# Linear attention inside a two-block layer: the exponents of the levels s = 32 and 64 taken from the running sum too, and running sums multiplied one head earlier

## What is computed

```python
b = jnp.cumsum(gc, axis=2)
rel = b[:, :, :, None, :] - b[:, :, None, :, :]
decay = jnp.exp(jnp.where(mask, rel, -jnp.inf))
attn = jnp.einsum('bhid,bhjd,bhijd->bhij', qc, kc, decay)
o = jnp.einsum('bhij,bhjv->bhiv', attn, vc) + jnp.einsum('bhid,bhdv->bhiv', qc * jnp.exp(b), state)
```

## Time and profile before

| | |
|---|---|
| median of 3 runs | 2332.88 us (2327.26 to 2337.95) |
| the profiled execution's own time | 2329.45 us |
| its span, first to last instruction | 2327.7 us |
| PE busy | 2269.9 us (98%) |
| DVE busy | 1671.5 us (72%) |
| ACT busy | 1117.6 us (48%) |
| POOL busy | 596.6 us (26%) |
| granted TensorE clock, mean | 0.997 |

### The profile page before, as it was taken

The page is one execution under the profiler, slowest core; times in us unless marked ns, Lnnn a source line. Parts: engine busy times, 40 slices in busy tenths (PEclk is TensorE's granted clock), DMA queues, the critical chain, the costliest instruction groups (busy, mean ns, idle before and its releaser), DMA issues.

```text
span 2327.7 us, 40250 instructions
## 1 busy us (share of the span) xinstructions
PE 2269.9 (98%) x14434; PEld 1352.6 (58%) x14434; DVE 1671.5 (72%) x3037; ACT 1117.6 (48%) x1755; POOL 596.6 (26%) x469
## 2 busy tenths in 40 slices
PE   8999999999999999999999999999999999999998
PEld 4448657555555666655555555564444465445885
DVE  6337765678999899968888888877453458777246
ACT  4267535666566788843333333344422234333234
POOL 0011213777787622233222222113000010000011
PEclk9999999999999999999999999999999999999999
DMA  6300034788888679989999999923333333333322
GB/s 201 93 10 1 2 98 131 247 294 306 310 307 296 219 268 356 355 320 396 372 358 358 364 358 361 368 72 112 92 114 100 100 98 104 100 104 108 101 73 73
DMA packets 164575, 471.26 MB, mean 202 GB/s; under 512 B 16800, under 2 KB 71712, under 8 KB 163680
## 3 DMA queue, kind: packets, MB, share of 16 engines
q1 hardware_dynamic: 109008, 289.94, 37.7%
q0 software_dynamic: 36864, 134.23, 15.5%
q10 hardware_dynamic: 18576, 45.36, 4.9%
HBM read 421.49 MB, written 47.45 MB: 201 GB/s over the span
## 4 chain that ended last, share of the span: by engine, by line
PE 76%; DVE 13%; ACT 3%; DMA 2%; POOL 2%; issue 2%; DVEq 1%; POOLq 0%; SPq 0%; ACTq 0%
PE psum L692 23%; PE psum L694 23%; PE psum L693 23%; DVE arena L2587 3%; DMA arena<-in_urows,arena 2%; DVE arena L666 1%; DVEq L2512 1%; POOL arena L672 1%; PE psum L1211 1%; ACT arena L653 1%; PE psum L1084 1%; PE psum L1379 1%; PE psum L1181 1%; PE psum L1380 1%; POOL arena L3001 1%
## 5 line engine op out<-in xcount | busy, mean ns | idle before, releaser
L692 PE MATMUL psum<-arena 128*128 128x384 f16 (+4 forms) x3968 | 1304.7, 330 | 20.0 <-POOL arena L672 4.9
L693 PE MATMUL psum<-arena 128*128 128x384 f16 (+4 forms) x3968 | 1308.2, 330 | 0.0
L694 PE MATMUL psum<-arena 128*128 128x384 f16 (+4 forms) x3968 | 1301.9, 330 | 0.0
L692 PEld LDWEIGHTS psum<-arena 128*128 128x128 f16 x3968 | 384.6, 97 | 309.5 <-issue 16.7
L694 PEld LDWEIGHTS psum<-arena 128*128 128x128 f16 x3968 | 383.6, 97 | 287.8 <-issue 1.1
L693 PEld LDWEIGHTS psum<-arena 128*128 128x128 f16 x3968 | 383.7, 97 | 278.7 <-issue 0.8
L666 DVE SCALAR_TENSOR_TENSOR arena<-arena 128x1024 f16<-128x1024 f32 x216 | 264.9, 1231 | 250.7 <-ACT arena L653 250.2
L653 ACT ACTIVATE arena<-arena 128x1024 f16<-128x1024 f32 x216 | 226.4, 1051 | 219.8 <-PE psum L694 170.8
L2031 ACT ACTIVATE arena<-arena 128x1024 f16<-128x1024 f32 x128 | 135.3, 1057 | 301.3 <-PE psum L694 287.3
L672 POOL TENSOR_TENSOR arena<-arena 128x1024 f16<-128x1024 f32 x104 | 229.8, 2210 | 78.8 <-ACT arena L661 77.7
L3001 POOL DMA_INDIRECT arena<-in_v,arena x128 | 129.3, 1010 | 359.9 <-DVE arena L2598 328.1
(11 more groups left out here) (290 smaller groups left out, 2275.9 us busy)
## 6 DMA issues: line engine op xcount, KB each, us to landing
arena<-in_w SPq DMA_DIRECT2D x320, 512.0 KB, 3.9
arena<-in_v SPq DMA_DIRECT2D x128, 512.0 KB, 6.0
early_activations<-arena ACTq DMA_DIRECT2D x124, 192.0 KB, 5.2
arena<-early_activations SPq DMA_DIRECT2D x124, 192.0 KB, 6.0
gate_matrix<-arena ACTq DMA_DIRECT2D x5, 4096.0 KB, 18.5
arena<-gate_matrix SPq DMA_DIRECT2D x32, 640.0 KB, 8.3
arena<-in_xT SPq DMA_DIRECT2D x4, 528.0 KB, 5.2
arena<-in_urows,arena POOLq DMA_INDIRECT x128, 6.9
```

Source lines behind the costliest of these rows:

```text
L692: nc.tensor.matmul(ps, a_h, b_h, start=first, stop=False)
L693: nc.tensor.matmul(ps, a_h, b_l, start=False, stop=False)
L694: return nc.tensor.matmul(ps, a_l, b_h, start=False, stop=last)
```

## The change

All seven levels within a tile, 0 to 6, go the way of the running sum (`NARROW` = 7): TensorE no longer multiplies sums for the levels 5 and 6 (16 matmuls a head, 64 in all), and GpSimd subtracts for 7 levels a head instead of 5, in the order of use (`SUB_ORDER`: 6, 0, 1, 2, 3, 4, 5). The running sums of the heads 0 and 1 are multiplied ahead of the levels' loop, that of head h + 2 behind head h. META's sums move from before the first unit of a head to before its third (`ISSUED` {2: META, 5: level 7, 7: level 8}).

```diff
-        NARROW = 5
-        EXP_ORDER = (STEPS[0], PREFIX, *STEPS[1:])
-        AHEAD = (META, NARROW, NS, NS + 1, STEPS[0], PREFIX)
-        PRODUCTS = [(0, STEPS[0]), (0, PREFIX), *((h + n // 4, li) for h in range(HEADS) for n, li in enumerate(AHEAD)
-                                                  if h + n // 4 < HEADS)]
-        ISSUED = {0: 0, 2: 1, 5: 2, 7: 3, 8: 4}
+        NARROW = NS
+        SUB_ORDER = LEVEL_ORDER[:NARROW]
+        EXP_ORDER = [(0, PREFIX), (1, PREFIX)]
+        for h in range(HEADS):
+            EXP_ORDER += [*((h, li) for li in STEPS), *([(h + 2, PREFIX)] if h + 2 < HEADS else [])]
+        AHEAD = (META, NS, NS + 1, PREFIX)
+        PRODUCTS = [(h, li) for h, li in EXP_ORDER if li in AHEAD]
+        ISSUED = {2: META, 5: NS, 7: NS + 1}
...
-                    if i in ISSUED and 2 + 6 * h + ISSUED[i] < len(PRODUCTS):
-                        exponents(2 + 6 * h + ISSUED[i])
+                    if i in ISSUED:
+                        exponents(PRODUCTS.index((h, ISSUED[i])))
...
-                if h < HEADS - 1:
-                    exponents(2 + 6 * h + 5)
+                if h + 2 < HEADS:
+                    exponents(PRODUCTS.index((h + 2, PREFIX)))
...
             turn_copy(HEADS * TT - 2)
-            step_exp(0)
+            prefix_copy(0)
             turn_copy(HEADS * TT - 1)
...
-            prefix_copy(0)
+            prefix_copy(1)
             head_out(HEADS - 1)
...
-            for n in range(1, HEADS * NSTEP + 3):
+            for n in range(HEADS * NSTEP + 3):
                 h, p = divmod(n, NSTEP)
                 if n < HEADS * NSTEP:
                     step_exp(n)
-                    if p == 0:
-                        prefix_copy(h)
+                    if p == NSTEP - 1 and h + 2 < HEADS:
+                        prefix_copy(h + 2)
...
-                for li in range(NARROW):
+                for li in SUB_ORDER:
                     n, s = narrow(h, li) - 1, LEVELS[li]
-                    if li == 0:
+                    if li == SUB_ORDER[0]:
                         pool.wait_ge(e_exp, exped(h, PREFIX))
```

More of the change, by code:

```diff
@@ L778, in exped @@
         def exped(h, li):
-            return h * len(EXP_ORDER) + EXP_ORDER.index(li) + 1
+            return EXP_ORDER.index((h, li)) + 1
         def narrow(h, li):
-            return h * NARROW + li + 1
+            return h * NARROW + SUB_ORDER.index(li) + 1
         keys_in, pq_out, s_done, s_out, head_done, gsub_out, gexp_out = (
@@ L1248, in _ @@
                                  stop=True).then_inc(wide_done, 1)
-            pe.wait_ge(e_exp, HEADS * len(EXP_ORDER))
+            pe.wait_ge(e_exp, exped(HEADS - 1, NS + 1))
             head_sums(1, A[0], range(HEADS - 1))
@@ L1881, in _ @@
                     nc.scalar.activation(xh[:, p // 2, 0:T], otmp[:, p // 2, :], ACT.Copy).then_inc(mixh_out, 1)
-                if p == 0:
+                if p == 0 and h >= 1:
                     pair_copy(h - 1)
@@ L2440, in _ @@
                     if h == 0 and p == 1:
-                        dve.wait_ge(e_exp, exped(0, PREFIX))
+                        dve.wait_ge(e_exp, exped(1, PREFIX))
                         nc.vector.tensor_tensor(KTm[0:DH], gk[0:DH, :, T:TM], v3(Emm, HEADS)[0:DH],
@@ L2982, in _ @@
                     if n >= len(subs):
-                        pool.wait_ge(e_exp, exped(*divmod(n - len(subs), NARROW)))
+                        pool.wait_ge(e_exp, exped((n - len(subs)) // NARROW, SUB_ORDER[(n - len(subs)) % NARROW]))
                     x = paired(prefix[h % 2], s)
```

## The result

The changed kernel takes 2347.47 us (median of 13 runs, 2336.15 to 2354.25), the kernel before took 2332.66 us in the 13 runs beside it (2327.26 to 2341.36): ratio 1.0054 [1.004, 1.0067] (the quotient of the medians, 1.0063, lies in that interval). The forecast was 2332.8 us with an upper end of 2338.5 us: it is wrong, the kernel became slower.

What follows compares the result with a forecast made beforehand. TensorE, busy for 98% of 2327.7 us, was taken as the bound; +1.1 - 0.2 - 0.4 - 0.3 - 0.6 + 0.3 = -0.1 us on the profiled 2329.45, plus 3.43 to the median, gave 2332.8 us, range 2326.5 to 2338.5 us.

Steps and rivals of the forecast that it cites:

- meetings: A POOL subtraction running beside a DVE product: two in head 0 at 0.15 us each, nothing in heads 1 to 3.
- start of head 0, without the hold: Level 6's exponential now needs running sum, copy and subtraction, so head 0's first units run later: +1.1 us.
- end of head 0, start of head 1: Passage from head 0 to 1: -0.2 us for dropped sums, -0.1 us for META's sums replacing level 5's.
- end of head 1, start of head 2: One group of sums dropped, -0.2 us; META's sums moved, -0.1, and ACT's copies sooner, -0.25 us.
- end of head 2, start of head 3: Both groups of sums dropped, -0.2 us; META's sums moved, -0.1, and ACT's copies sooner, -0.35 us.
- their 4.4 us: PE time of the 64 dropped matmuls, 8 groups of 0.55 us; forecast to be mostly not gained.
- Rival A: PE's own time decides, so the dropped sums count in full: -4.3 us, 2328.6 us; chance 0.17.
- POOL beside DVE: Subtractions now fall beside DVE's products: +0.3 us in head 0 (between 0 and 2.1), nothing in heads 1 to 3.
- the forecast's own sign against itself: If the products at line 2348 lengthen beyond 0.9 us, the forecast is wrong and the slower rival holds.
- The cover in heads 1 to 3: DVE's waits for PE at each step (0.17 us in one row) hide meetings, up to about 0.5 us a head.
- rival B: POOL's subtractions hold DVE's products of levels 1, 2 and 3: +3.7 us (2336.5) to +9.6 us (2342); chance 0.16.
- two groups stood around unit 7, of level 6 and of PREFIX: Sums at a head's end; dropping one or both gives -0.2 us, as level 8 waits for DVE.

Runs made afterwards that it cites:

- 1: Changed kernel with GpSimd's 28 subtractions left out, exponentials reading the running sum itself: 2330.46 us, ratio 1.0.
- 7: Changed kernel with head 0's level 6 from TensorE's sums again and each subtraction waiting for DVE's product three before it: 2329.6 us, ratio 0.9996.
- 10: Changed kernel with only the two subtractions a head at the passages between heads waiting for DVE's product: 2335.17 us, ratio 1.0016.
- looks 5 and 6: Changed kernel without any edit, profiled twice more to see slower executions: 2351.31 and 2354.36 us, both at clock 0.987.
- 2: Changed kernel with each subtraction from the fourth on waiting for DVE's product three before it, not for ACT's exponential: 2335.4 us, ratio 1.0009.
- 3: Changed kernel with head 0's level 6 made from TensorE's sums in PSUM again, undoing the late start: 2342.76 us, ratio 1.0053.
- 11: Changed kernel with only the five subtractions a head away from the passages waiting for DVE's product: 2347.18 us, ratio 1.0074.
- 9: Changed kernel with 24 of the 64 dropped matmuls put back at their old places, read by nobody: 2335.8 us, ratio 1.0029.
- look 1: First of two further profiles of the changed kernel, without any edit: 2351.31 us at clock 0.987.

## Why the prediction was wrong

**What held.** Compared with the kernel without meetings (1), the terms come out nearly as summed.

| term | forecast, us | measured, us | from |
|---|---|---|---|
| start of head 0, without the hold | +1.1 | +1.2 | 1 against before, second masked copy (16.91 for 15.71) |
| end of head 0, start of head 1 | -0.2 - 0.1 | -0.36 | head 1 of 1 |
| end of head 1, start of head 2 | -0.2 - 0.35 | -0.65 | head 2 of 1, 7 and after |
| end of head 2, start of head 3 | -0.2 - 0.45 | -0.65 | head 3 of 1, 7 and 10 |

That the sums do not bring their 4.4 us is also right. Rival A is out: the whole of the gain in run 7 is 1.7 us. At the passage from head 1 to 2 ACT's copy of level 8 begins at 274.29 us, as PE ends META's unit, as forecast. And where no meeting fell on the end of a head, level 8 begins 1.5 us behind the unit of level 5, as forecast, with TensorE released by DVE: at the end of head 1, whose unit of level 5 begins at 269.55,

```profile
272.16 0.48 PE L1244 MATMUL psum<-arena 64*128 64x256 f32 x1 [0.45 <-DVE arena L2348]
```

(269.55 + 1.04 + 1.57 = 272.16; 1.55 with the signal was the forecast). The unit of level 6 of head 0 begins at 227.13, which is 226.4 without the 0.7 us from ahead of the stretch; the forecast had 225.8, and 0.5 us of the difference is a held product.

**The step that failed** is "*POOL beside DVE*": "In heads 1 to 3 ... I cost it at nothing" and "In head 0 ... two meetings at 0.15 us". A meeting costs up to 0.86 us (1.53 - 0.67), not 0.15, and the forecast's own sign against itself, products beyond 0.9 us, is there. The 0.19 us that I priced it by came from a subtraction that was about to end (0.31 us to go); the placement that the same paragraph foresaw, one step behind each product, has the subtraction begin 0.1 us (261.67 before 261.79) to 0.5 us (290.64 before 291.13) ahead of DVE's instruction, so that half to nearly all of its 1.04 us is still to come. The Trainium skill, page "SBUF — State Buffer", section "SBUF: two separate sides", says that the loser blocks for the whole of the other's instruction; the 1.47 us of 261.79 agree with that, and I had weighed it below a row that did not show the case. Nor did that row speak against the rule as I took it to: its product too ended 0.55 us behind the subtraction (273.58 for 273.03), and so lost 0.12 us less than was left (0.19 of 0.31), as in the long meetings (0.80 of 0.92, 0.42 of 0.55). Two more things of that step were wrong. The cover in heads 1 to 3 is 0.17 to 0.25 us a step in head 2, but in head 1 DVE runs without waits: so head 1 paid 2.0 us (24.45 for 22.48), head 3 0.6, head 0 0.5 at its start, and head 2 nothing, though its products of 279.82 and 281.95 us took 1.10 and 1.47. And not only products are held: a small scale of 64x256 went from 0.35 to 1.24 us.

The meetings come to 0.5 + 2.0 + 0.6 = 3.1 us. This is rival B, which was put at +3.7 to +9.6 us over the forecast, of 4.0 us and more in meetings: even its near end was somewhat high, but far nearer than the forecast's 0.3. Its median of 2336.5 us missed for the same reason as the forecast's: neither held the clock.

**The step that was missing** is the clock. The forecast costed the end of head 2 as a change of what TensorE waits for, "two groups stood around unit 7, of level 6 and of PREFIX", and took their absence as a gain of 0.2 us. It did not ask what else their presence did. With them TensorE had no wait at this place; without them and with a held product it idles for 1.4 us, and in 7 of 13 runs the mean clock was 0.991 or less; in the two further executions of looks 5 and 6 some 37.5 us at 1.2 GHz begin right there and cost 15.6 us up to the output projection in the second. That is the size of the 14.8 us between the medians. Taking away the hold at the passage ends it: with a wait of 1.0 us (1, 2, 7, 10) none of 47 runs is at 0.991 or less, with the hold and the idle time (after, 3, 11) 18 of 31. Taking away the idle time (9: wait 0.2 us) leaves 3 of 12, which points the same way without showing it. A second, shorter half-clock piece, 3.3 us in head 0, comes with the late start and costs 1.6 us of the profiled execution.

For the profiled execution the sum should have read: +1.2 + 0.5 (start and its hold) + 1.6 (half clock in head 0) - 1.65 (passages) + 2.0 + 0.6 (meetings) = +4.2 us, which is the 92.42 - 88.21 of the stretch. (It has to come out, as the terms are differences of these same lengths; what supports it is that each length comes back in other kernels.)

**What stays open.** What decides, run by run, whether the clock falls at the end of head 2: waits of the same length stand in profiles of either kind, in look 1 and run 9 a piece begins in head 1 behind shorter waits, and with the filler three runs still fell. Why half-clock pieces stand in the expert stage of the profile after is not explained either, nor is the wait that takes back run 7's gain. No version that was run beats the kernel before by more than its measurement can tell.

## What to carry to other kernels

- Before GpSimd work is moved or released by another engine's progress, place each of its instructions beside VectorE's next one with two SBUF inputs: if it begins ahead, charge what it still has to do (here less 0.12 us). Price such a meeting by a row in which the other instruction has just begun, not by one in which it is ending. Releasing it by VectorE's own last product, so that it runs beside an operation that reads PSUM, made it free in heads 1 to 3 here with a one-line edit.
- Matmuls that seem superfluous may be what keeps TensorE from a wait, as the two groups at the end of head 2 did. When work is dropped ahead of a wait, ask how long TensorE now idles there, and what the next tens of microseconds would cost at half its clock; look at the granted clock of every run, not of the profiled one alone.
- Measure a periodic stretch by the same instruction in each period. Here the lengths of four heads separated three effects that the total had mixed.

## What the hardware showed that was not expected

- A wait of 1.43 us can be followed by 37.5 us at the 1.2 GHz level, during which TensorE is busy for nearly all of the time (39.46 of 40 us in look 1) with small float32 matmuls for the most part. In look 1 TensorE had been busy for 17.82 of the 20 us before (275 to 295 us, granted clock 1.00), the wait among them. A wait of 1.0 us at the same place was followed by no mean clock of 0.991 or less in 47 runs.
- Both engines can lose. GpSimd's subtraction goes from 1.04 to 1.57 us when VectorE's product has begun first; VectorE's product goes from 0.67 to 1.53 us when the subtraction has. VectorE's masked copies with PSUM inputs (1.32 us) and the subtractions beside them are not lengthened at all.
